# Low parts of the summed output weights written over the sums, four raw buffers in rotation, fewer DVE operations for the activation sums, residual loaded by token tiles

## The chip, the cores and the metric

One core of one Trainium2 chip (trn2) runs the whole block. The metric is the device time in microseconds of one execution; shown is the median of three runs. The engines are named as the profile names them: PE (TensorE), DVE (VectorE), ACT (ScalarE), POOL (GpSimd) and SP (SyncE, here only an issuer of DMAs).

## The reference, cut to what matters

The layer normalises `x` (512 tokens x 2048), projects it, runs two attention branches, gates both, and ends with an output projection, a residual sum and an RMSNorm. The change lies in this last part:

```python
mixed = jnp.concatenate([out_a, out_b], axis=-1)           # 512 x 2048
x = x + jnp.einsum('bsc,cd->bsd', mixed, w_out)            # w_out 2048 x 2048
return rms_norm(x, final_norm_w)
```

All of it is float32. PE gets a float32 product from three faster ones: each operand is split into a high part (rounded) and a low part (the rest), and `hi*hi + hi*lo + lo*hi` is summed. Every operand of PE so costs one copy by ACT (high) and one subtraction by DVE or POOL (low).

## The kernel before, in words

`mixed` is held transposed, 16 tiles of 128 columns x 512 tokens, as eight pairs `j`. The output has 2048 columns. The first 1024 are made plainly: 16 chunks of weights (`WO0 + s`) go through `w_raw`, `w_hi` and `w_lo`, and PE accumulates four token tiles (`out_chunks`, end signalled by `o_done`). The last 1024 columns are made by a product of 2x2 blocks with seven multiplications in place of eight. The operands are sums of blocks:

- of the activations, `unit_sums(j)` (three sums, `u_sum`) and `pair_sums(j)` (two differences, `p_sum`), each then split by `unit_high`/`unit_low` and `pair_high`/`pair_low`;
- of the weights, in 16 **visits** `v`. Visit `v` loads 1 MB, four blocks of 128x512, from `w_pairs` into a raw buffer `t_raw`; `part_sums(v)` (DVE) sums blocks in place (one operation of 128x1024, from visit 8 on one more of 128x512); `part_high(v, g)` (ACT) writes `t_hi`; `part_low(v, g)` (DVE) writes `t_lo`; PE multiplies. Group `g` = 0 is what PE reads first, `g` = 1 what it reads after.

PE takes 18 matmuls in each of visits 0 to 7, 24 in each of 8 to 13, and 48 for the visits 14 and 15 together: 336. In visit 8 it needs the banks that visit 7 has left, so it waits for `y_added`: DVE adds them to the residual `y` in eight operations, `add`, which stand in its order behind `part_low(8, 1)`.

The order on each engine is the order of the code. DVE's is `part_low(v,0)`, `part_sums(v+1)`, `part_low(v,1)`. There are two buffers each of `t_raw`, `t_hi` and `t_lo`. SP loads visit `v` once both low parts of visit `v-2` are made:

```python
for v in range(2, VISITS):
    sp.wait_ge(t_low[0], v - 1)
    sp.wait_ge(t_low[1], v - 1)
    sp.dma_start(t_raw[v % 2][:, :, :], w_pairs[v, :, :, :]).then_inc(t_landed[v % 2], 16)
```

ACT issues the loads of the residual `x_nat` (four of 1 MB, by 512 columns) and of the final gains (`fw`), and squares finished pieces of `y` (`square`). POOL multiplies finished 128x512 pieces of `y` by the gains (`gained`, L393) once they are squared; the first four of these that concern the visits wait for `fws_landed`, all three loads of `fw[1:4]`. At the end DVE adds the last banks, and row by row the norm is applied and stored.

Of the kernel before, what the change touches and what calls it, by code (L numbers as in the profile page):

```python
# [14 lines left out]
P = 128  # L15
# [17 lines left out]
CE = 1024  # L33
# [67 lines left out]
def build(nc, w_stream, w_pairs, x_t, x_nat, gains, final_w, tables, out):  # L101
    with ExitStack() as ctx:
# [10 lines left out]
        def at(name, shape, dt, offset):  # L113
            return nc.alloc_sbuf_tensor_at(name, shape, dt, offset=offset)
# [27 lines left out]
        w_lo = at("w_lo", [P, HL, CE], F32R, r_lo)  # L142
        t_raw = [at("t_raw0", [P, 4, PART], F32, r_x + 56 * KB), at("t_raw1", [P, 4, PART], F32, r_raw)]
        t_hi = [at(f"t_hi{par}", [P, 4, PART], F32R, r_hi + 8 * KB * (1 - par)) for par in range(2)]
        t_lo = [at(f"t_lo{par}", [P, 4, PART], F32R, r_lo + 8 * KB * (1 - par)) for par in range(2)]

# [97 lines left out]
        def part_slots(v, g):  # L244
            return slice(0, 2) if g == 1 else slice(3, 4) if v < 8 else slice(2, 4)

# [17 lines left out]
        y0_landed, y1_landed, y_landed, fw_landed, fws_landed = sem("y0_landed"), sem("y1_landed"), sem("y_landed"), sem("fw_landed"), sem("fws_landed")  # L264
        t_landed = [sem("t_landed0"), sem("t_landed1")]
        u_summed, u_high, u_low, p_summed, p_high, p_low = sem("u_summed"), sem("u_high"), sem("u_low"), sem("p_summed"), sem("p_high"), sem("p_low")
# [25 lines left out]
        def _(sp):  # L292
# [122 lines left out]
        def _(act):  # L415
# [267 lines left out]
            def unit_high(j):  # L683
                act.wait_ge(u_summed, 3 * j + 3)
                act.activation(u_hi[j][:, :, :], u_sum[j % 2][:, :, :], ACT.Copy).then_inc(u_high, 1)

            def pair_high(j):
                act.wait_ge(p_summed, 2 * j + 2)
                act.activation(dead(mx_hi[j]), p_sum[:, j % 2, :, :, :], ACT.Copy).then_inc(p_high, 1)

            def part_high(v, g):

                if g == 0 and v < 8:
                    act.wait_ge(t_landed[v % 2], 16 * (v // 2) + 16)
# [12 lines left out]
                s = part_slots(v, g)  # L707
                act.activation(t_hi[v % 2][:, s, :], t_raw[v % 2][:, s, :], ACT.Copy).then_inc(t_high, 1)  # L708

# [70 lines left out]
        def _(dve):  # L780
# [400 lines left out]
            def unit_sums(j):  # L1181

                if j >= 2:
                    dve.wait_ge(u_low, j - 1)
                even, odd = by_tile(mixed, 2 * j), by_tile(mixed, 2 * j + 1)
                for n, (a, b) in enumerate(((even[:, :, 0, :], odd[:, :, 1, :]), (even[:, :, 1, :], odd[:, :, 1, :]), (even[:, :, 0, :], odd[:, :, 0, :]))):
                    dve.tensor_tensor(u_sum[j % 2][:, n, :].rearrange("p (q c) -> p q c", q=2), a, b, ALU.add).then_inc(u_summed, 1)  # L1187

# [20 lines left out]
            def part_sums(v):  # L1209

                raw = t_raw[v % 2]
                dve.wait_ge(t_landed[v % 2], 16 * (v // 2) + 16)
                dve.tensor_tensor(raw[:, 0:2, :], raw[:, 0:2, :], raw[:, 2:4, :], ALU.subtract if v < 8 else ALU.add).then_inc(t_summed, 1)  # L1213
                if v >= 8:
# [103 lines left out]
            for q in range(2):  # L1318
# [19 lines left out]
        def _(pe):  # L1338
# [523 lines left out]
```

## Time and profile before

| what | value |
|---|---|
| median of 3 runs | 718.03 us (717.88 to 718.6) |
| the profiled execution's own time | 716.37 us |
| its span, first to last instruction | 714.6 us |
| mean granted TensorE clock | 0.979 |
| busy: PE, DVE, ACT, POOL | 93%, 62%, 46%, 38% of the span |

The page cuts the span into 40 slices of 17.9 us. Each digit is the busy share of a slice in tenths (9 is 90% or more), PEclk the granted clock in tenths:

```profile
PE   9999999999999999999999999999999986569853
DVE  5868053896945546455456687765376973457565
PEclk9999999999999999999999999999999999989988
DMA  8633322322222222223223212202462273333315
```

PE is full until slice 32, which ends at 590 us, and has gaps from there on: those are the 16 visits. A "releaser" in a row is what ended an idle time.

### The profile page before, as it was taken

Reading aid. Unit: us, or ns where it says so; the run is one execution under the profiler, and the core shown is the slowest. Engines: PE = TensorE matmul, PEld = TensorE weight load, DVE = VectorE, ACT = ScalarE, POOL = GpSimd, SP = SyncE. Lnnn points to the kernel's source line nnn. Section 1 sums busy time; section 2 is a strip of 40 time slices with the busy share of each in tenths; the row PEclk is TensorE's granted clock in tenths of the full one; section 3 lists DMA queues with packets and bytes.
Section 4 is the critical chain, followed back from the end, with each engine's and each line's share of the span. In section 5 each row is a group of like instructions: output and inputs, shape, how many; then the busy total and the mean of one; then the engine's idle time right before and its main releaser. Section 6 shows DMA issues by size and latency. Waiting matters only on the chain.

```text
span 714.6 us, 8810 instructions
## 1 busy us (share of the span) xinstructions
PE 665.7 (93%) x3126; PEld 553.4 (77%) x3126; DVE 443.8 (62%) x720; ACT 332.0 (46%) x622; POOL 272.6 (38%) x132
## 2 busy tenths in 40 slices
PE   9999999999999999999999999999999986569853
PEld 8888888888888888888888898888888864347642
DVE  5868053896945546455456687765376973457565
ACT  6841232213245636645546676885542341222225
POOL 0054451644344234433342566677747202001001
PEclk9999999999999999999999999999999999989988
DMA  8633322322222222223223212202462273333315
GB/s 288 249 118 99 108 89 88 118 89 91 86 91 87 89 89 88 66 84 117 89 67 110 90 60 89 69 22 88 152 246 71 78 258 139 117 132 143 137 60 236
DMA packets 22169, 81.96 MB, mean 115 GB/s; under 512 B 2417, under 2 KB 2673, under 8 KB 20081
## 3 DMA queue, kind: packets, MB, share of 16 engines
q1 hardware_dynamic: 18000, 73.41, 29.7%
q10 hardware_dynamic: 4128, 8.02, 3.2%
q8 instruction: 25, 0.41, 0.2%
q14 instruction: 16, 0.12, 0.1%
HBM read 77.22 MB, written 4.19 MB: 114 GB/s over the span
## 4 chain that ended last, share of the span: by engine, by line
PE 77%; DVE 11%; DMA 8%; issue 1%; ACT 1%; DVEq 0%; SPq 0%; ACTq 0%
PE bank L1341 23%; PE bank L1344 22%; PE bank L1345 22%; DMA t_raw<-w_pairs 8%; DVE t_lo L1221 3%; DVE t_raw L1213 3%; PE bank L1606 1%; DVE y L1234 1%; DVE u_sum L1187 1%; DVE p_sum L1203 1%; PE bank L1485 1%; PE bank L1495 1%; DVE t_raw L1216 1%; PE bank L1592 1%; PE bank L1593 1%
## 5 line engine op out<-in xcount | busy, mean ns | idle before, releaser
L328 POOL TENSOR_TENSOR w_lo<-w_raw,w_hi 128x1024 fp32r<-128x1024 f32 x84 | 206.0, 2457 | 270.4 <-ACT w_hi L421 270.2
L1341 PE MATMUL bank<-x_hi,w_hi 128*128 128x512 f32 x496 | 193.7, 391 | 0.0
L1344 PE MATMUL bank<-x_hi,w_lo 128*128 128x512 f32 x496 | 193.3, 390 | 0.0
L1345 PE MATMUL bank<-x_lo,w_hi 128*128 128x512 f32 x496 | 193.2, 390 | 0.0
L421 ACT ACTIVATE w_hi<-w_raw 128x1024 fp32r<-128x1024 f32 x93 | 98.2, 1056 | 130.5 <-PE bank L1341 109.0
L1345 PEld LDWEIGHTS bank<-x_lo,w_hi 128*128 128x128 f32 x496 | 93.1, 188 | 19.7
L1341 PEld LDWEIGHTS bank<-x_hi,w_hi 128*128 128x128 f32 x496 | 93.2, 188 | 18.7 <-DVE mixed L1039 0.3
L1344 PEld LDWEIGHTS bank<-x_hi,w_lo 128*128 128x128 f32 x496 | 93.2, 188 | 18.1
L393 POOL TENSOR_TENSOR y<-y,fw 128x512 f32<-128x512 f32 x12 | 18.0, 1519 | 134.2 <-ACT junk L681 108.0
L708 ACT ACTIVATE t_hi<-t_raw 128x1024 fp32r<-128x1024 f32 (+1 forms) x32 | 29.4, 945 | 77.3 <-DVE t_raw L1216 47.7
L1341 PE MATMUL bank<-t_hi,mx_hi 128*128 128x512 f32 x64 | 28.8, 450 | 24.9 <-DVE t_lo L1221 24.9
L1341 PE MATMUL bank<-w_hi,mx_hi 128*128 128x512 f32 x128 | 50.3, 393 | 0.0
L1345 PE MATMUL bank<-w_lo,mx_hi 128*128 128x512 f32 x128 | 49.9, 390 | 0.0
L1344 PE MATMUL bank<-w_hi,mx_lo 128*128 128x512 f32 x128 | 49.9, 390 | 0.0
L1213 DVE TENSOR_TENSOR t_raw<-t_raw 128x1024 f32<-128x1024 f32 x16 | 20.4, 1278 | 43.8 <-DMA t_raw<-w_pairs 43.8
L519 ACT ACTIVATE bank<-pa,st_a 128x128 f32<-128x128 f32 x64 | 22.8, 356 | 43.3 <-DVE st_a L953 43.3
L1341 PEld LDWEIGHTS bank<-t_hi,mx_hi 128*128 128x128 f32 x64 | 13.3, 208 | 32.3 <-DVE t_lo L1221 29.7
L1221 DVE TENSOR_TENSOR t_lo<-t_raw,t_hi 128x1024 fp32r<-128x1024 f32 (+1 forms) x32 | 35.2, 1120 | 4.0 <-ACT t_hi L708 4.0
L968 DVE TENSOR_TENSOR pta_lo<-bank,pta_hi 128x512 fp32r<-128x512 f32 x16 | 11.1, 692 | 32.1 <-ACT pta_hi L526 32.0
L1341 PE MATMUL bank<-t_hi,u_hi 128*128 128x512 f32 x48 | 20.3, 422 | 11.2 <-DVE t_lo L1221 6.5
L1345 PEld LDWEIGHTS bank<-w_lo,mx_hi 128*128 128x128 f32 x128 | 24.0, 188 | 5.0
L856 DVE TENSOR_TENSOR t<-bank,sin_r 32x512 f32<-32x512 f32 x40 | 27.5, 687 | 0.5
(239 smaller groups left out, 1250.5 us busy)
## 6 DMA issues: line engine op xcount, KB each, us to landing
w_raw<-w_stream SPq DMA_DIRECT2D x93, 512.0 KB, 3.3
t_raw<-w_pairs SPq DMA_DIRECT2D x15, 1024.0 KB, 4.8
y<-x_nat ACTq DMA_DIRECT2D x4, 1024.0 KB, 6.0
out<-y SPq DMA_DIRECT2D x8, 512.0 KB, 3.1
xs<-x_t SPq DMA_DIRECT2D x4, 512.0 KB, 5.3
mixed<-x_t SPq DMA_DIRECT2D x4, 512.0 KB, 6.0
t_raw<-w_pairs ACTq DMA_DIRECT2D x1, 1024.0 KB, 7.7
fw<-final_w ACTq DMA_DIRECT2D x4, 256.0 KB, 4.7
```

What stands on the lines that cost most here:

```text
L328: pool.tensor_tensor(w_lo[:, s % HL, :], w_raw[:, s % RAW, :], w_hi[:, s % HL, :].bitcast(F32), ALU.subtract)\
L393: pool.tensor_tensor(y[:, t, cols], y[:, t, cols], fw[n][:, :], ALU.mult).then_inc(o_gained, 1)
L421: act.activation(w_hi[:, s % HL, :], w_raw[:, s % RAW, :], ACT.Copy).then_inc(w_hi_ready, 1)
L519: act.activation(B[4][:, P * k:P * k + P], pa[:, slot, k, :], ACT.Exp, bias=st[:, 1, k:k + 1], scale=A_SCALE, accum_out=st[:, 3, k:k + 1])
L708: act.activation(t_hi[v % 2][:, s, :], t_raw[v % 2][:, s, :], ACT.Copy).then_inc(t_high, 1)
L856: ins = dve.tensor_tensor(t2[32 * q:32 * q + 32, :], src[32 * o:32 * o + 32, :], sin[32 * q:32 * q + 32, :], ALU.mult)
L968: dve.tensor_tensor(pta_lo[:, :], B[6][:, :], pta_hi[:, :].bitcast(F32), ALU.subtract).then_inc(a_pt_lo, 1)
L1213: dve.tensor_tensor(raw[:, 0:2, :], raw[:, 0:2, :], raw[:, 2:4, :], ALU.subtract if v < 8 else ALU.add).then_inc(t_summed, 1)
L1221: dve.tensor_tensor(t_lo[v % 2][:, s, :], t_raw[v % 2][:, s, :], t_hi[v % 2][:, s, :].bitcast(F32), ALU.subtract).then_inc(t_low[g], 1)
L1341: ins = pe.matmul(dst, ah, bh, start=start, stop=False, skip_group_check=goes_on)
L1344: pe.matmul(dst, al, bh, start=False, stop=False, skip_group_check=goes_on)
L1345: return pe.matmul(dst, ah, bl, start=False, stop=stop, skip_group_check=goes_on)
```

## The change: what it does

- **Raw buffers.** `t_raw` has four buffers. `t_lo` has four as well, and each lies on the bytes of the `t_raw` of the same number: the low part is written over the sum it is made from. `t_hi` keeps two. To make that fit, the sums are written into blocks 2 and 3, and the order of blocks in `w_pairs` is changed on the host; two `add` operations become subtractions.
- **Loads of the visits.** SP loads visit 2 when PE has begun chunk 14 of the plain part, visit 3 when PE has ended the plain part, and visit `v` from 4 on when PE has ended visit `v-4`.
- **Activation sums.** `unit_sums` is two operations (128x512 with a broadcast operand, and 128x256) in place of three of 128x256; `pair_sums` is one of 128x512 in place of two of 128x256.
- **Residual.** The second half of the columns is loaded by pairs of token tiles: tiles 2 and 3 behind `unit_high(2)`, tiles 0 and 1 where both loads stood.
- **Final gains.** ACT issues the three loads of `fw[1:4]` behind `part_high(6, 1)`; they stood behind `part_high(1, 1)`.

```diff
-        t_raw = [at("t_raw0", [P, 4, PART], F32, r_x + 56 * KB), at("t_raw1", [P, 4, PART], F32, r_raw)]
+        t_at = [r_x + 56 * KB, r_raw, r_lo + 8 * KB, r_lo]
+        t_raw = [at(f"t_raw{n}", [P, 4, PART], F32, o) for n, o in enumerate(t_at)]
+        t_lo = [at(f"t_lo{n}", [P, 4, PART], F32R, o) for n, o in enumerate(t_at)]
...
-            for v in range(2, VISITS):
-                sp.wait_ge(t_low[0], v - 1)
-                sp.wait_ge(t_low[1], v - 1)
-                sp.dma_start(t_raw[v % 2][:, :, :], w_pairs[v, :, :, :]).then_inc(t_landed[v % 2], 16)
+            sp.wait_ge(w_used, WO0 + 14)
+            sp.dma_start(t_raw[2][:, :, :], w_pairs[2, :, :, :]).then_inc(t_landed[2], 16)
+            sp.wait_ge(o_done, 8)
+            sp.dma_start(t_raw[3][:, :, :], w_pairs[3, :, :, :]).then_inc(t_landed[3], 16)
+            for v in range(4, VISITS):
+                if v == 11:
+                    sp.wait_ge(m_done, 6)
+                else:
+                    sp.wait_ge(t_used, 2 * v - 6 if v < 11 else 2 * v - 8)
+                sp.dma_start(t_raw[v % 4][:, :, :], w_pairs[v, :, :, :]).then_inc(t_landed[v % 4], 16)
...
+            def residual_rows(t):
+                act.dma_start(y[:, t:t + 2, CE:], x_nat[0, P * t:P * t + 2 * P, CE:].rearrange("(t p) d -> p t d", p=P)).then_inc(y_landed, 16)
...
             unit_high(2)
+            residual_rows(2)
             high_part(WO0 + 10, WO0 + 10)
...
             act.wait_ge(u_low, 8)
-            residual_in(2, y_landed)
-            residual_in(3, y_landed)
+            residual_rows(0)
             part_high(1, 0)
             pair_high(7)
             part_high(1, 1)
-            act.wait_ge(p_low, 8)
-            for n in range(1, 4):
-                act.dma_start(fw[n][:, :], final_w[:, SEQ * n:SEQ * n + SEQ]).then_inc(fws_landed, 16)
...
                 part_high(v, 0)
                 part_high(v, 1)
+                if v == 6:
+                    act.wait_ge(p_low, 8)
+                    for n in range(1, 4):
+                        act.dma_start(fw[n][:, :], final_w[:, SEQ * n:SEQ * n + SEQ]).then_inc(fws_landed, 16)
...
-                    dve.tensor_tensor(u_sum[j % 2][:, n, :].rearrange("p (q c) -> p q c", q=2), a, b, ALU.add).then_inc(u_summed, 1)
+                dve.tensor_tensor(u_sum[j % 2][:, 0:2, :].rearrange("p n (q c) -> p n q c", q=2), even.rearrange("p q e c -> p e q c"),
+                                  odd[:, :, 1, :].unsqueeze(1).to_broadcast([P, 2, 2, P]), ALU.add).then_inc(u_summed, 1)
+                dve.tensor_tensor(u_sum[j % 2][:, 2, :].rearrange("p (q c) -> p q c", q=2), even[:, :, 0, :], odd[:, :, 0, :], ALU.add).then_inc(u_summed, 1)
...
-                dve.tensor_tensor(p_sum[:, j % 2, 0, :, :], even[:, :, 1, :], even[:, :, 0, :], ALU.subtract).then_inc(p_summed, 1)
-                dve.tensor_tensor(p_sum[:, j % 2, 1, :, :], odd[:, :, 0, :], odd[:, :, 1, :], ALU.subtract).then_inc(p_summed, 1)
+                both = mixed[:, 2 * j:2 * j + 2, :].rearrange("p k (q e c) -> p k q e c", q=2, e=2)
+                dve.tensor_tensor(p_sum[:, j % 2, :, :, :], both[:, :, :, 1, :], both[:, :, :, 0, :], ALU.subtract).then_inc(p_summed, 1)
```

What the edits do to the order is seen at three places. The first is SP's queue where the visits' loads begin, before (`t_low0`, `t_low1` count the low parts of groups 0 and 1 made by DVE):

```order
L308 ISA [waits w_lo_ready]
L308 DMA w_raw<-w_stream 128x1024
...
L311 DMA t_raw_61<-w_pairs 128x2048 [waits w_lo_ready]
L315 DMA t_raw_60<-w_pairs 128x2048 [waits t_low1,t_low0]
L315 DMA t_raw_61<-w_pairs 128x2048 [waits t_low1,t_low0]
```

and now (`t_used` counts the groups PE has ended; 60 to 63 are the raw buffers):

```order
L312 DMA t_raw_61<-w_pairs 128x2048 [waits w_lo_ready]
L314 DMA t_raw_62<-w_pairs 128x2048 [waits w_used]
L316 DMA t_raw_63<-w_pairs 128x2048 [waits o_done]
L322 DMA t_raw_60<-w_pairs 128x2048 [waits t_used]
L322 DMA t_raw_61<-w_pairs 128x2048 [waits t_used]
L322 DMA t_raw_62<-w_pairs 128x2048 [waits t_used]
```

The number and order of the loads are as before; what each waits for has changed from DVE to PE, two visits further back. The second place is ACT's order at the visits 1 and 2, before:

```order
L671 DMA y<-x_nat 128x4x512 x2
L708 ACTIVATE t_hi_63<-t_raw_61 128x512
L689 ACTIVATE mx_hi_134<-p_sum 128x2x2x128
L708 ACTIVATE t_hi_63<-t_raw_61 128x1024
L748 DMA fw_165<-final_w 128x512
L748 DMA fw_166<-final_w 128x512
L748 DMA fw_167<-final_w 128x512
L681 ACTIVATE junk,sumsq<-y 128x512 x4
```

and now, down to visits 6 and 7:

```order
L681 DMA y<-x_nat 128x2x1024
L718 ACTIVATE t_hi_69<-t_raw_61 128x512
L699 ACTIVATE mx_hi_138<-p_sum 128x2x2x128
L718 ACTIVATE t_hi_69<-t_raw_61 128x1024
L691 ACTIVATE junk,sumsq<-y 128x512 x4
...
L718 ACTIVATE t_hi_68<-t_raw_62 128x1024
L765 DMA fw_169<-final_w 128x512
L765 DMA fw_170<-final_w 128x512
L765 DMA fw_171<-final_w 128x512
L718 ACTIVATE t_hi_69<-t_raw_63 128x512
```

One load of the residual has left this place, and the three loads of the gains stand five visits later. The third is DVE's order while PE is in the plain part, before (the sums of pair 2 and of unit 4, then their low parts):

```order
L1202 TENSOR_TENSOR p_sum<-mixed 128x256
L1203 TENSOR_TENSOR p_sum<-mixed 128x256
L1187 TENSOR_TENSOR u_sum_145<-mixed 128x256 x3
L1207 TENSOR_TENSOR mx_lo_137<-p_sum,mx_hi_129 128x2x2x128
L1191 TENSOR_TENSOR u_lo_160<-u_sum_145,u_hi_152 128x768
```

and now:

```order
L1214 TENSOR_TENSOR p_sum<-mixed 128x512
L1197 TENSOR_TENSOR u_sum_149<-mixed 128x512
L1199 TENSOR_TENSOR u_sum_149<-mixed 128x256
L1218 TENSOR_TENSOR mx_lo_141<-p_sum,mx_hi_133 128x2x2x128
L1203 TENSOR_TENSOR u_lo_164<-u_sum_149,u_hi_156 128x768
```

Five sums of one place are now three; nothing has changed its turn.

## Rows read from the trace of the kernel before

**Rows 1.** The page, chain that ended last, shares of the span by engine.

```profile
PE 77%; DVE 11%; DMA 8%; issue 1%; ACT 1%; DVEq 0%; SPq 0%; ACTq 0%
```

**Rows 2.** Busy time by stretch (stretch, length, engines, PEclk, DMA share, GB/s).

```profile
577.40:702.90 125.50, 89.39 (x337) 67.82 (x336) 73.88 (x85) 38.75 (x55) 10.83 (x7) 0.90 0.40 142
590.00:600.00 10.00, 4.62 (x15) 3.40 (x14) 4.04 (x3) 1.69 (x2) 4.76 (x4) 0.83 0.32 120
```

**Rows 3.** Waits from 577.6 to 702.9 us (in total, times, longest).

```profile
DVE t_raw L1213 <- DMA t_raw<-w_pairs: 43.8, 12, 4.4
...
PE bank L1341 <- DVE t_lo L1221: 31.4, 14, 5.4
```

**Rows 4.** The chain in order of time (start, length, what), in the visits.

```profile
585.29 7.10 DMA t_raw<-w_pairs
...
603.13 4.84 DMA t_raw<-w_pairs
608.00 1.23 DVE t_raw L1213
609.22 1.15 DVE t_lo L1221
```

**Rows 5.** PE's instructions in order of time (start, length, idle before).

```profile
577.21 0.39 PE L1345 MATMUL bank<-w_lo,mx_hi 128*128 128x512 f32 x1
...
582.21 0.50 PE L1341 MATMUL bank<-t_hi,u_hi 128*128 128x512 f32 x1 [0.53 <-DVE t_lo L1221]
...
585.27 0.50 PE L1341 MATMUL bank<-t_hi,mx_hi 128*128 128x512 f32 x1 [1.40 <-DVE t_lo L1221]
...
588.86 0.50 PE L1341 MATMUL bank<-t_hi,u_hi 128*128 128x512 f32 x1 [0.58 <-DVE t_lo L1221]
...
595.90 0.80 PE L1341 MATMUL bank<-t_hi,mx_hi 128*128 128x512 f32 x1 [5.38 <-DVE t_lo L1221]
...
598.99 0.40 PE L1344 MATMUL bank<-t_hi,mx_lo 128*128 128x512 f32 x1
...
642.12 0.80 PE L1341 MATMUL bank<-t_hi,u_hi 128*128 128x512 f32 x1 [4.67 <-DVE y L1234]
...
697.02 0.39 PE L1345 MATMUL bank<-t_lo,mx_hi 128*128 128x512 f32 x1
...
702.46 0.39 PE L1345 MATMUL bank<-t_lo,mx_hi 128*128 128x512 f32 x1
```

**Rows 6.** Instructions on `t_raw`: ns min/median/max, first and last start.

```profile
L1221 DVE TENSOR_TENSOR t_lo<-t_raw,t_hi x32: 678/1218/2296, 570.5 to 690.4; 128x1024 fp32r<-128x1024 f32 x24, 128x512 fp32r<-128x512 f32 x8
L1213 DVE TENSOR_TENSOR t_raw<-t_raw x16: 1218/1226/2090, 564.2 to 686.2; 128x1024 f32<-128x1024 f32 x16
...
L1216 DVE TENSOR_TENSOR t_raw<-t_raw x8: 691/692/1664, 631.2 to 687.5; 128x512 f32<-128x512 f32 x8
```

**Rows 7.** DVE's instructions in order of time.

```profile
578.41 2.48 DVE L1226 TENSOR_TENSOR y<-bank,y 128x512 f32<-128x512 f32 x4
...
640.79 4.87 DVE L1234 TENSOR_TENSOR y<-y,bank 128x512 f32<-128x512 f32 x8
...
652.80 2.09 DVE L1213 TENSOR_TENSOR t_raw<-t_raw 128x1024 f32<-128x1024 f32 x1 [0.66 <-DMA t_raw<-w_pairs]
654.92 1.66 DVE L1216 TENSOR_TENSOR t_raw<-t_raw 128x512 f32<-128x512 f32 x1
```

**Rows 8.** POOL's instructions in order of time.

```profile
588.75 6.01 POOL L393 TENSOR_TENSOR y<-y,fw 128x512 f32<-128x512 f32 x4 [26.18 <-DMA fw<-final_w]
652.52 3.52 POOL L393 TENSOR_TENSOR y<-y,fw 128x512 f32<-128x512 f32 x2 [57.76 <-ACT junk L681]
699.85 1.30 POOL L393 TENSOR_TENSOR y<-y,fw 128x512 f32<-128x512 f32 x1 [43.82 <-ACT junk L681]
```

**Rows 9.** ACT's instructions and DMA issues in order of time.

```profile
539.85 1.06 ACT L421 ACTIVATE w_hi<-w_raw 128x1024 fp32r<-128x1024 f32 x1 [3.33 <-PE bank L1341]
...
582.98 1.31 ACTq L748 DMA_DIRECT2D fw<-final_w  x3
```

More of the change, by code:

```diff
@@ L244, in part_slots @@
         def part_slots(v, g):
-            return slice(0, 2) if g == 1 else slice(3, 4) if v < 8 else slice(2, 4)
+            return slice(2, 4) if g == 1 else slice(1, 2) if v < 8 else slice(0, 2)
         def dead(mx):
@@ L264, in build @@
         y0_landed, y1_landed, y_landed, fw_landed, fws_landed = sem("y0_landed"), sem("y1_landed"), sem("y_landed"), sem("fw_landed"), sem("fws_landed")
-        t_landed = [sem("t_landed0"), sem("t_landed1")]
+        t_landed = [sem(f"t_landed{n}") for n in range(4)]
         u_summed, u_high, u_low, p_summed, p_high, p_low = sem("u_summed"), sem("u_high"), sem("u_low"), sem("p_summed"), sem("p_high"), sem("p_low")
@@ L683, in unit_high @@
             def unit_high(j):
-                act.wait_ge(u_summed, 3 * j + 3)
+                act.wait_ge(u_summed, 2 * j + 2)
                 act.activation(u_hi[j][:, :, :], u_sum[j % 2][:, :, :], ACT.Copy).then_inc(u_high, 1)
             def pair_high(j):
-                act.wait_ge(p_summed, 2 * j + 2)
+                act.wait_ge(p_summed, j + 1)
                 act.activation(dead(mx_hi[j]), p_sum[:, j % 2, :, :, :], ACT.Copy).then_inc(p_high, 1)
@@ L693, in part_high @@
                 if g == 0 and v < 8:
-                    act.wait_ge(t_landed[v % 2], 16 * (v // 2) + 16)
+                    act.wait_ge(t_landed[v % 4], 16 * (v // 4) + 16)
                 else:
@@ L707, in part_high @@
                 s = part_slots(v, g)
-                act.activation(t_hi[v % 2][:, s, :], t_raw[v % 2][:, s, :], ACT.Copy).then_inc(t_high, 1)
+                act.activation(t_hi[v % 2][:, s, :], t_raw[v % 4][:, s, :], ACT.Copy).then_inc(t_high, 1)
             act.sem_inc(o_squared, 1)
@@ L1209, in part_sums @@
             def part_sums(v):
[L1211 to L1214, printed above, removed]
+                raw = t_raw[v % 4]
+                dve.wait_ge(t_landed[v % 4], 16 * (v // 4) + 16)
+                if v < 8:
+                    dve.tensor_tensor(raw[:, 2:4, :], raw[:, 0:2, :], raw[:, 2:4, :], ALU.subtract).then_inc(t_summed, 1)
+                else:
+                    dve.tensor_tensor(raw[:, 2:4, :], raw[:, 2:4, :], raw[:, 0:2, :], ALU.add).then_inc(t_summed, 1)
                     dve.wait_ge(t_summed, 2 * v - 7)
-                    dve.tensor_tensor(raw[:, 2, :], raw[:, 2, :], raw[:, 3, :], ALU.add).then_inc(t_summed, 1)
+                    dve.tensor_tensor(raw[:, 0, :], raw[:, 0, :], raw[:, 1, :], ALU.add).then_inc(t_summed, 1)
             def part_low(v, g):
                 dve.wait_ge(t_high, 2 * v + g + 1)
+                if g == 0 and v < 8:
+                    dve.wait_ge(t_summed, v + 1)
                 s = part_slots(v, g)
-                dve.tensor_tensor(t_lo[v % 2][:, s, :], t_raw[v % 2][:, s, :], t_hi[v % 2][:, s, :].bitcast(F32), ALU.subtract).then_inc(t_low[g], 1)
+                dve.tensor_tensor(t_lo[v % 4][:, s, :], t_raw[v % 4][:, s, :], t_hi[v % 2][:, s, :].bitcast(F32), ALU.subtract).then_inc(t_low[g], 1)
             def residual(n, t):
@@ L1292, in _ @@
             for q in range(2):
-                add(2 * q + 1, 2, q, q + 5, 2 * q + 1)
+                add(2 * q + 1, 2, q, q + 5, 2 * q + 1, op=ALU.subtract)
             part_low(9, 0)
@@ L1330, in _ @@
                     scaled(0, 1, 3, 9)
-                add(2 * q, 2, q, d + 4, b + 5)
+                add(2 * q, 2, q, d + 4, b + 5, op=ALU.subtract)
             scaled(2, 3, 3, 10)
@@ L1697, in m @@
             def m(v, q, bk, s, slot, start=False):
-                return three(B[bk + q][:, :], *s, t_hi[v % 2][:, slot, :], t_lo[v % 2][:, slot, :], start, v in (7, 15), goes_on=v >= 8 and bk in (0, 6))
+                return three(B[bk + q][:, :], *s, t_hi[v % 2][:, slot, :], t_lo[v % 4][:, slot, :], start, v in (7, 15), goes_on=v >= 8 and bk in (0, 6))
             def m1(v, q):
-                return m(v, q, 4, s1(v - 8, q), 2, v == 8)
+                return m(v, q, 4, s1(v - 8, q), 0, v == 8)
             def m5(v, q):
-                return m(v, q, 2, s5(v - 8, q), 3, v == 8)
+                return m(v, q, 2, s5(v - 8, q), 1, v == 8)
             def m6(v, q):
-                return m(v, q, 6, s_kept(v - 8, q, 0, 1), 0)
+                return m(v, q, 6, s_kept(v - 8, q, 0, 1), 2)
             def m7(v, q):
-                return m(v, q, 0, s_kept(v - 8, q, 1, 0), 1)
+                return m(v, q, 0, s_kept(v - 8, q, 1, 0), 3)
             for v in range(8):
@@ L1717, in _ @@
                 for q in range(2):
-                    ins = m(v, q, 4, s2(v, q), 3, v == 0)
+                    ins = m(v, q, 4, s2(v, q), 1, v == 0)
                     if v == 7:
@@ L1726, in _ @@
                 for q in range(2):
-                    ins = m(v, q, 6, s_kept(v, q, 0, 0), 0, v == 0)
+                    ins = m(v, q, 6, s_kept(v, q, 0, 0), 2, v == 0)
                     if v == 7:
@@ L1732, in _ @@
                 for q in range(2):
-                    ins = m(v, q, 0, s_kept(v, q, 1, 1), 1, v == 0)
+                    ins = m(v, q, 0, s_kept(v, q, 1, 1), 3, v == 0)
                     if v == 7:
@@ L1816, in laid_out_pairs @@
     blocks = w_out[:, 2 * SEQ:].reshape(8, 2, P, 2, SEQ)
-    order = [((0, 1), (1, 0), (1, 1), (0, 0)), ((0, 1), (1, 0), (0, 0), (1, 1))]
+    order = [((0, 1), (0, 0), (1, 1), (1, 0)), ((0, 0), (1, 1), (0, 1), (1, 0))]
     return np.ascontiguousarray(np.concatenate([np.stack([blocks[:, k, :, n, :] for k, n in o], axis=2) for o in order], axis=0))
```

3 lines of the change are left out of this document (removed).

## The prediction

> **What bounds the kernel now.** I read the chain first: PE carries 77% of it, DVE 11% and DMA 8% [rows 1]. Eight per cent of 714.6 us is 57 us in which the end waited for a load, and the slices say where: PE is full up to about 580 us and has gaps behind. So next the busy times by stretch. From 577.4 to 702.9 us, the visits, PE is busy 89.39 of 125.5 us at a granted clock of 0.90, over 337 matmuls, one of them the last of the plain part [rows 2]: 36 us idle, and part of the rest run slowly. The waits name the cause: 31.4 us of PE's waits are for `t_lo`, and DVE itself waited 43.8 us for loads of `t_raw` [rows 3].
>
> The chain in order of time shows the loop: a load of 4.84 us, a sum of 1.23 us, a low part of 1.15 us, then the next load [rows 4]. With two buffers and DVE's order (sum of visit v+1 ahead of the second low part of visit v) a visit takes all three in a row, 7.3 us; from visit 8 on there is one more sum of 0.69 us [rows 6] and it takes 7.9. PE needs less. In the last stretch 24 steps from 697.02 to 702.46 us take 5.44 us, 0.2267 us a matmul [rows 5]: 18 matmuls are 4.08 us, 24 are 5.44. The visits are bound by the load's latency, not by its bandwidth.
>
> **The floor.** PE's visits start where its last plain matmul ends, 577.21 + 0.23 = 577.44 us [rows 5]. 336 matmuls x 0.2267 = 76.2 us. Before, PE ended at 702.46 + 0.39 = 702.85 us [rows 5], 125.4 us after its start: 49.2 us are waits and slow clock. That is all that can be had in the visits. The 11.75 us from PE's end to the end of the span (last adds, norms, stores) are not touched by the change and I keep them.
>
> **Four raw buffers.** Let PE end visit v at T. The load of visit v+4 goes out, lands at T+4.9, its sum is made by T+6.1, then the second low part of visit v+3 by T+7.3. PE starts visit v+3 at T+8.2 and wants that low part at T+9.5. Slack 2.2 us. In the visits from 8 on, the sums end at T+6.9 and the low part at T+8.1, wanted at T+13.6: slack 5.5. DVE has 1.23 + 0.69 + 1.22 = 3.1 us of work for a visit of 4.08 us, then 1.23 + 0.69 + 2 x 1.22 = 4.4 us for 5.44 [rows 6]. `t_hi` still has two buffers: from PE's end of a group ACT needs 1.06 and DVE 1.22 us, 2.4 in all with the signals, and PE comes back to that group 5.4 us later. So in the steady state nothing waits and PE sets the pace: 16 visits cost the 76.2 us. What is late next is what stands between the visits. In the order of time:
>
> 1. *Start.* Before, PE waited 0.53 + 1.40 + 0.58 = 2.5 us here [rows 5], since DVE reached the four residual sums at 578.41 us and ended them at 580.9 [rows 7], 3.4 us behind PE's last plain matmul. Three of the four can be made before PE ends; so DVE can gain up to 3.4 - 0.8 = 2.6 us, and no less than 0. Eight pairs and eight units lose an operation each on the way there, and an operation that meets one of POOL costs about 1 us more (1.66 in place of 0.69 us, [rows 7, 6], beside POOL's two of 652.52, [rows 8]); POOL makes low parts all along this stretch. I take DVE 1.5 us earlier. ACT, too, issues one load less and squares without first issuing the gains (1.31 us, [rows 9]). Waits left: 1.0 us, between 0 and 2.5.
>
> 2. *Visit 8.* Let T be the start of visit 7. Sums of visit 8, low parts (7,1) and (8,0) are made by T+1.2; the load of visit 9 has landed at T+0.8, its sums end at T+3.0, the low part (8,1) at T+4.2, and then come eight adds in 4.87 us [rows 7]. PE wants the second at T+5.4: it is there. The fourth costs it 0.5, visit 9's low part 0.2. That is 0.7 us in place of the 4.67 us that it waited here before [rows 5].
>
> 3. *POOL in the way.* The three loads of gains used to be issued at 583 us, so POOL's four products ran from 588.75 us for 6.01 us [rows 8], when DVE was waiting for a load. Now ACT issues them behind the high part (6,1), which waits for PE's end of visit 4 and takes the 1.06 us of a copy of this size [rows 9]. The issues take 1.31 us and the landing 588.75 - 584.29 = 4.5 us more, together 6.9 us after visit 4, or 1.3 us before visit 7. POOL then works beside DVE in the very stretch of step 2 where DVE has no slack. What a POOL product costs DVE, two rows show: a sum took 2.09 in place of 1.23 us and one 1.66 in place of 0.69 while POOL ran two products [rows 7, 8], 1.83 us for two, so 3.7 us for four. I take 3.7. Bounds: 0, if they fall into a pause, and 6.0, if each costs DVE all that a product takes beside other work (6.01/4 = 1.5 us).
>
> The Trainium skill, "SBUF — State Buffer", section "Who interferes with whom", says that a DVE instruction with two SBUF inputs and a POOL instruction that reads SBUF exclude each other for a whole instruction. By that rule four products of 1.30 us, the uncontended row, would cost 5.2 us and the end would come 1.5 us later than by the rows; the adds of step 2 (one input from PSUM) would go free. The trace agrees with the blocking, and shows 0.9 us per product, not 1.3.
>
> 4. *Visit 10.* Two more products of POOL behind the squares. DVE has 1 us of slack there and loses 1.8: 1.0 us, between 0 and 2.
>
> 5. *Visits 14 and 15.* PE reaches group 1 of visit 15 after only 12 matmuls of the pair; its high part must wait for the end of visit 13, and high and low part need 2.4 us, of which 1.36 are covered by PE. 1.2 us wait.
>
> 6. *Clock.* After the gap of 5.38 us PE ran the next 7 matmuls in 598.99 - 595.90 = 3.09 us in place of 1.59 [rows 5], in a stretch with granted clock 0.83 [rows 2], so partly at the lower of the two levels (1.2 GHz in place of 2.4). One gap of about 4 us is left, at visit 8: 1.5 us. Between 0 and 3.4.
>
> **Costs at nothing.** The early half of the residual (1 MB at about 527 us) can delay chunk loads. But at 539.85 ACT waits 3.33 us for PE to free a chunk's place, not for a load [rows 9]: the chunks are ahead. Without that cover it would cost a load's length, 5 us at most. The other half, visit 3's load and visit 4's are 3 MB within 4 us. The load of 7.10 us at 585.29 shows such a crowd [rows 4]; visit 3 is wanted 10 us and visit 4 9 us after issue. Writing a low part over its sum: L1213 writes in place already, at 1.226 us median against 1.218 for L1221, which does not [rows 6]. The flipped signs and the 4 KB runs of the residual: same operations, same bytes.
>
> **The sum.** 76.2 + 1.0 + 0.7 + 3.7 + 1.0 + 1.2 + 1.5 = 85.3 us of visits, against 125.4. PE ends at 662.7, the span is 662.7 + 11.75 = 674.5, 40.1 us less than 714.6. The execution's own time of 716.37 becomes 676.3; the median of the runs lies 1.66 us above it, 718.03, and becomes 677.9 us.
>
> **Rivals.**
> - *POOL does not touch DVE's path.* For it: before, the four products of 588.75 us lay in a pause of DVE, which waited for the load that ended at 592.4 [rows 4, 8]. Against: that pause is what the change takes away. Steps 3, 4 and 6 fall: 677.9 - 6.2 = 671.7; with half of step 4 kept, 672.
> - *Loads get slower.* Now up to three are under way, and each row of 4.84 us was alone. If one takes the 7.10 us of the crowded row, the slack of 2.2 us in visits 3 to 8 is gone, visit 9's load lands at T+3.1 and the adds are 2.3 us late; if in turn they only run one behind the other at 4.84 against PE's 4.08, seven visits lose 0.76 each, 5.3 less the slack of 2.2. Both come to about +3, 681. Against: 142 GB/s over the stretch [rows 2], and 1 MB in 4.08 us is 257.
> - *DVE becomes the bound, and the kernel slower.* Low parts written over their own input, with a broadcast operand and PE reading the same lines, could run slower than the two-buffer form. DVE's work in the visits is 8 x 3.1 + 8 x 4.4 = 60 us plus 4.9 of adds. To use up 125.4 us its operations must take 2.0 times as long; at 2.1 times it is 131 us and the time 723. For it: factors of 1.7 to 2.4 do occur, beside POOL. Against: POOL is busy 10.8 us in the whole stretch, and in-place costs nothing in rows 6.
> - *The buffers free nothing*, because `t_hi` still has two: excluded by 2.4 against 5.4 us above, so I give it next to nothing; it would be 718.
>
> **Chances.** My forecast 0.58; POOL harmless 0.22; slower loads 0.17; no change 0.01; slower 0.02. The bounds of the steps give 677.9 - 7.2 = 670.7 below (1.0, 3.7, 1.0 and 1.5 all gone) and, above, +1.5 for the start, +2.3 for POOL, +1 for visit 10, +1.9 for the clock and +2 for loads: 686.6. This takes in the first two rivals. Faster by over 0.2% (about what a measurement of this kernel can tell from no change): 0.97; within: 0.01; slower: 0.02.
>
> **What would show it.** Right: DVE's waits for `t_raw` loads fall from 43.8 us to under 10; PE's for `t_lo` from 31.4 to under 5; in visits 3 to 7 no PE gap, a visit each 4.1 us, from 8 on each 5.4 to 5.5; a gap of 3 to 5 us in visit 8 released by DVE's `y`, beside four POOL products; clock at 1.00 but behind that gap; loads issued at PE's visit ends. Wrong: gaps in every visit, loads above 7 us, DVE operations on `t_raw` above 1.3 us without POOL, or a tail after PE's end that is not 11.75 us.

## The result, and the profile after

| | before | after |
|---|---|---|
| median | 717.95 us (717.27 to 718.6, 4 runs) | 678.08 us (677.9 to 678.47, 4 runs) |
| the profiled execution's own time, its span | 716.37, 714.6 us | 678.47, 676.7 us |
| PE's visits, first matmul to the end of the last | 577.44 to 702.85 us | 577.91 to 665.03 us |

The ratio is 0.9445 (95%: 0.9429 to 0.9462). Forecast were 677.9 us.

The slices of the page after, now 16.9 us each, and its chain that ended last:

```profile
PE   9999999999999999999999999999999999997993
DVE  5958031978784635645544578777545489879975
PEclk9999999999999999999999999999999999997997
DMA  8732222233122212222321412202127523683516
...
PE 87%; DVE 7%; issue 2%; ACT 2%; DMA 1%; DVEq 0%; ACTq 0%
```

PE carries 87% of the chain in place of 77%, and DMA 1% in place of 8% [rows 1]. One slice, the 37th, is left with a visible gap.

The stretch of the visits but for its last 2 us, and the 20 us around that gap (columns as in [rows 2]):

```profile
577.40:663.00 85.60, 79.27 (x331) 63.42 (x331) 73.28 (x78) 37.37 (x52) 12.63 (x7) 0.96 0.51 185
610.00:620.00 10.00, 5.93 (x22) 4.46 (x22) 9.96 (x10) 2.00 (x2) 5.27 (x3) 0.86 0.53 182
620.00:630.00 10.00, 10.00 (x37) 7.99 (x36) 8.80 (x10) 3.35 (x6) 1.40 (x1) 0.79 0.29 107
```

DVE has 73 us of work in both kernels [rows 2], once in 125.5 us and now in 85.6. The waits in this stretch (in total, times, longest):

```profile
PE bank L1356 <- DVE y L1249: 4.1, 1, 4.1
DVE t_raw L1225 <- DMA t_raw<-w_pairs: 2.6, 2, 1.4
DVE t_raw L1227 <- DMA t_raw<-w_pairs: 2.4, 1, 2.4
PE bank L1356 <- DVE t_lo L1236: 2.1, 3, 1.1
```

DVE's waits for loads are 5.0 us in place of 43.8, PE's for `t_lo` 2.1 in place of 31.4 [rows 3]. All of PE's idle times of 0.2 us and more in the visits:

```profile
583.74 0.50 PE L1356 MATMUL bank<-t_hi,mx_hi 128*128 128x512 f32 x1 [0.23 <-DVE t_lo L1236]
...
609.75 0.50 PE L1356 MATMUL bank<-t_hi,mx_hi 128*128 128x512 f32 x1 [0.79 <-DVE t_lo L1236]
...
618.20 0.79 PE L1356 MATMUL bank<-t_hi,u_hi 128*128 128x512 f32 x1 [4.07 <-DVE y L1249]
...
655.19 0.50 PE L1356 MATMUL bank<-t_hi,mx_hi 128*128 128x512 f32 x1 [1.11 <-DVE t_lo L1236]
```

How the gap at 618.20 comes about, in the chain of waits (start, length, what), in DVE's rows and in POOL's:

```profile
599.47 6.01 DMA t_raw<-w_pairs
```
```profile
605.51 1.23 DVE L1227 TENSOR_TENSOR t_raw<-t_raw 128x1024 f32<-128x1024 f32 x1 [2.37 <-DMA t_raw<-w_pairs]
...
607.38 4.54 DVE L1236 TENSOR_TENSOR t_lo<-t_raw,t_hi 128x1024 fp32r<-128x1024 f32 x2
611.85 2.31 DVE L1227 TENSOR_TENSOR t_raw<-t_raw 128x1024 f32<-128x1024 f32 x1
614.19 1.63 DVE L1229 TENSOR_TENSOR t_raw<-t_raw 128x512 f32<-128x512 f32 x1
615.74 1.21 DVE L1236 TENSOR_TENSOR t_lo<-t_raw,t_hi 128x1024 fp32r<-128x1024 f32 x1
616.88 4.86 DVE L1249 TENSOR_TENSOR y<-y,bank 128x512 f32<-128x512 f32 x8
```
```profile
607.23 8.04 POOL L400 TENSOR_TENSOR y<-y,fw 128x512 f32<-128x512 f32 x4 [44.59 <-DMA fw<-final_w]
```

The load for visit 8 is late (6.01 us), then DVE's operations that start from 607.38 to 614.19 are long: these are the ones beside POOL's four products. Behind the gap PE is slow for 14 matmuls, of which these are two:

```profile
618.79 0.63 PE L1359 MATMUL bank<-t_hi,u_lo 128*128 128x512 f32 x1
619.22 0.63 PE L1360 MATMUL bank<-t_lo,u_hi 128*128 128x512 f32 x1
```

They start 0.43 us apart, up to 623.91 us, in place of 0.23. The granted clock of this stretch is 0.50, the lower of the two levels (1.2 GHz):

```profile
618.20:624.00 5.80, 5.80 (x14) 4.47 (x15) 5.80 (x9) 0.00 (x0) 0.00 (x0) 0.50 0.01 3
```

### The profile page after: what moved, and what is told of

The parts are those of the page before. It is cut to its first block, busy times and chain, and to the rows that moved or that the text cites. A ratio compares the mean times of both kernels' runs of the same rounds, so it can differ in the third digit from the quotient of the medians.

```text
span 676.7 us, 8788 instructions
## 1 busy us (share of the span) xinstructions
PE 657.6 (97%) x3126; PEld 550.7 (81%) x3126; DVE 442.1 (65%) x704; ACT 332.2 (49%) x622; POOL 274.9 (41%) x132
## 4 chain that ended last, share of the span: by engine, by line
PE 87%; DVE 7%; issue 2%; ACT 2%; DMA 1%; DVEq 0%; ACTq 0%
PE bank L1356 26%; PE bank L1359 26%; PE bank L1360 26%; DVE t_lo L1236 2%; PE bank L1621 1%; PE bank L1500 1%; PE bank L1510 1%; DMA t_raw<-w_pairs 1%; DVE y L1249 1%; DVE p_sum L1214 1%; ACT junk L691 1%; DVE u_lo L1203 1%; PE bank L1386 1%; PE bank L1607 1%; PE bank L1608 1%
## 5 line engine op out<-in xcount | busy, mean ns | idle before, releaser
L400 POOL TENSOR_TENSOR y<-y,fw 128x512 f32<-128x512 f32 x12 | 20.6, 1738 | 94.2 <-ACT junk L691 49.6
L1236 DVE TENSOR_TENSOR t_lo<-t_raw,t_hi 128x1024 fp32r<-128x1024 f32 (+1 forms) x32 | 37.3, 1187 | 5.3 <-ACT t_hi L718 5.3
L1356 PE MATMUL bank<-t_hi,mx_hi 128*128 128x512 f32 x64 | 26.2, 410 | 2.3 <-DVE t_lo L1236 2.1
L1356 PEld LDWEIGHTS bank<-w_hi,mx_hi 128*128 128x128 f32 x128 | 24.0, 188 | 4.7
L1359 PEld LDWEIGHTS bank<-w_hi,mx_lo 128*128 128x128 f32 x128 | 24.1, 188 | 4.6
L987 DVE TENSOR_TENSOR mixed<-bank,o_low 64x256 f32<-64x256 f32 x32 | 13.5, 422 | 21.6 <-ACT o_low L540 21.4
```

The costliest lines, as they stand in the source:

```text
L400: pool.tensor_tensor(y[:, t, cols], y[:, t, cols], fw[n][:, :], ALU.mult).then_inc(o_gained, 1)
L987: ins = dve.tensor_tensor(out_e, by_head[h, e], o_low[h, :, :, :], ALU.add)
L1236: dve.tensor_tensor(t_lo[v % 4][:, s, :], t_raw[v % 4][:, s, :], t_hi[v % 2][:, s, :].bitcast(F32), ALU.subtract).then_inc(t_low[g], 1)
L1356: ins = pe.matmul(dst, ah, bh, start=start, stop=False, skip_group_check=goes_on)
L1359: pe.matmul(dst, al, bh, start=False, stop=False, skip_group_check=goes_on)
```

## The experiments

In the table "waits" are PE's idle times in the visits that the profile puts down to another engine (0.15 us and more). "Slow" are the matmuls that start 0.3 to 0.7 us after the one before them without such a wait, with what they take beyond 0.2267 us each, and the last column has those among them that lie in or right behind a stretch with a granted clock of 0.50. Most of the others are the second matmul behind a wait: it starts 0.33 to 0.35 us after the first, at a granted clock of 1.00, and so costs 0.11 us. All this is worked out from PE's rows of the one profiled execution. The ratio is to the runs of before on the same chip.

| kernel | median | ratio (95%) | visits | waits | slow | of these, clock |
|---|---|---|---|---|---|---|
| before | 717.95 | 1 | 125.4 | 36.1 | 54: 10.1 | 42: 8.8 |
| after | 678.08 | 0.9445 (0.9429 to 0.9462) | 87.1 | 6.2 | 20: 3.7 | 14: 2.9 |
| e1 buffers only | 678.06 | 0.9447 (0.9429 to 0.9466) | 86.1 | 7.1 | 9: 1.0 | 0 |
| e2 gains early | 677.05 | 0.9425 (0.9401 to 0.9448) | 86.8 | 6.5 | 16: 2.5 | 8: 1.6 |
| e3 gains late | 675.0 | 0.9405 (0.9388 to 0.9422) | 83.2 | 4.6 | 8: 0.9 | 0 |
| e4 no products | 675.59 | 0.9406 (0.9386 to 0.9426) | 84.6 | 4.5 | 16: 2.6 | 9: 1.6 |
| e5 order, two buffers | 689.36 | 0.9601 (0.9579 to 0.9622) | 98.5 | 15.1 | 29: 5.4 | 21: 4.5 |
| e6 sums only | 716.51 | 0.9981 (0.997 to 0.9993) | 125.4 | 33.2 | 68: 12.9 | 59: 12.0 |
| e7 three buffers | 688.78 | 0.9598 (0.9577 to 0.9618) | 97.9 | 13.4 | 36: 6.4 | 24: 4.9 |
| e8 paced products | 672.77 | 0.9387 (0.9358 to 0.9415) | 81.4 | 2.3 | 11: 1.5 | 0 |
| e9 paced, order swapped | 680.48 | 0.9481 (0.9459 to 0.9503) | 88.7 | 7.8 | 20: 3.6 | 15: 3.0 |

**e1: the four buffers alone.** Before, with SP's rotation and the low parts over the sums; the sums of the activations, the residual and the place of the gains' loads stay as they were.

```diff
-        t_raw = [at("t_raw0", [P, 4, PART], F32, r_x + 56 * KB), at("t_raw1", [P, 4, PART], F32, r_raw)]
+        t_raw = [at(f"t_raw{n}", [P, 4, PART], F32, o) for n, o in enumerate(t_at)]
+        t_lo = [at(f"t_lo{n}", [P, 4, PART], F32R, o) for n, o in enumerate(t_at)]
```

> Only the four raw buffers with the low parts over the sums and the loads at PE's visit ends; the activation sums, the residual loads and the place of the gains' loads are those of before. Theory (the buffers carry the gain; the late gains cost something that the other edits give back): 76.2 us of matmuls, 2.5 of waits at the start, about 1.5 where POOL's four products now meet the low slack of visits 3 and 4, 0.7 at visit 8, 1.0 and 1.2 at visits 10 and 15, no slow clock: PE ends 42 us earlier than before, 674 to 679 us. Rival (the activation sums and the residual carry a good part): 683 us or more.

678.06 us, the same as after and in the theory's range. So the buffers are enough for the whole gain, and the other edits add up to nothing that the runs can tell. They do not do nothing: the start here waits as before (0.53, 1.41 and 0.58 us, [rows 5], and 0.62 more in visit 2) where after waits 0.23, and visits 4 and 10 wait 0.74 and 1.92 us where after doesn't. Against that, visits 7 and 8 cost 0.22 us where after waits 4.86 and then runs at the lower clock for 2.9. What the other edits gain at the start, the later loads of the gains take back. The edit of the residual was never run by itself.

**e2 and e3: the gains' loads earlier and later.** After, with the three loads of `fw` where they were before (behind `part_high(1, 1)`), and, in e3, behind visit 11.

```diff
-                if v == 6:
+                if v == 11:
```

> The changed kernel with the three loads of the gains back behind part_high(1,1). Theory (at visit 8 it is POOL's products and the crowded load that hold DVE up): the gap of 4.07 us at visit 8 falls to about 0.7, the slow clock behind it (14 matmuls at 0.43 us, 2.8 us) goes, and POOL costs up to 1.5 us at visits 3 and 4: 671 to 674 us. Rival (DVE's own order, low part and eight adds, makes the gap): visit 8 keeps over 3 us and the time stays at 677 to 680.

> The changed kernel with the three loads of the gains behind part_high(11,1). Theory (as for the early place, and DVE has 5.5 us of slack a visit from 10 on): no gap at visit 8 over 1 us, none made at visits 12 to 14: 670 to 673 us, below the early place. Rival (POOL's six products then run into the tail, where the products are waited for): over 677 us.

Both fell short of what was expected. POOL's products of e2, and PE beside them:

```profile
590.70 7.93 POOL L400 TENSOR_TENSOR y<-y,fw 128x512 f32<-128x512 f32 x4 [28.18 <-DMA fw<-final_w]
```
```profile
599.77 0.50 PE L1355 MATMUL bank<-t_hi,mx_hi 128*128 128x512 f32 x1 [1.75 <-DVE t_lo L1235]
...
631.26 0.50 PE L1355 MATMUL bank<-t_hi,mx_hi 128*128 128x512 f32 x1 [1.95 <-DVE t_lo L1235]
```

Visit 8 waits 0.23 us, as expected, but the products in a row now cost 1.75 us at visit 4, and visit 10 waits 1.95 us, which after doesn't. In e3 all six products run in one row, beside visits 11 to 13:

```profile
631.19 11.82 POOL L400 TENSOR_TENSOR y<-y,fw 128x512 f32<-128x512 f32 x6 [69.15 <-DMA fw<-final_w]
```
```profile
644.14 0.50 PE L1356 MATMUL bank<-t_hi,mx_hi 128*128 128x512 f32 x1 [2.23 <-DVE t_lo L1236]
...
649.49 0.50 PE L1356 MATMUL bank<-t_hi,u_hi 128*128 128x512 f32 x1 [1.65 <-DVE t_lo L1236]
```

The damage moves with the products. The median of e2 can't be told from after's (the intervals of the ratios overlap), and it lies in the rival's range although the rival's gap at visit 8 is not there. e3 is 3.1 us below after, with intervals that don't overlap: the place matters, even with six products in a row.

**e4: without the four products.** After, but POOL only signals; columns 512 to 1023 of the output lack their final gain.

```diff
-                gained(t, 1)
+                pool.sem_inc(o_gained, 1)
```

> The changed kernel; POOL leaves out the four products of the second column quarter by the gains (output columns 512 to 1023 lack the final gain). The loads of the gains stay behind part_high(6,1). Theory (the four products cost DVE about 4 us, which all come out as PE's wait): the gap of 4.07 us falls to 1 to 1.5 us, the rest being the load of visit 8 that takes 6.0 in place of 4.8 us beside the loads of the gains; with the slow clock 672 to 674 us. Rival (the gap is the crowded load's alone): the gap stays above 3 us, 677 us.

```profile
613.65 0.50 PE L1356 MATMUL bank<-t_hi,u_hi 128*128 128x512 f32 x1 [1.01 <-DVE y L1249]
614.85 0.50 PE L1356 MATMUL bank<-t_hi,u_hi 128*128 128x512 f32 x1 [0.23 <-DVE y L1249]
...
628.78 0.50 PE L1356 MATMUL bank<-t_hi,mx_hi 128*128 128x512 f32 x1 [1.95 <-DVE t_lo L1236]
```

The waits up to visit 8 are now 1.24 us in place of 4.86 (0.79 in visit 7 and 4.07 in visit 8): the four products cost PE 3.6 us. What is left follows the load of visit 8: with 1.24 us of waits here it takes 6.02 us beside the gains' loads, and where these stand elsewhere, in e2 and e3, it takes 4.7 us and the visit waits 0.23 and 0.21. So 1.0 of the 1.24 us is the crowded load. The expected time was missed because the wait of visit 10 comes back, as in e2: the two other products start at 624.04 us, and the gap in which DVE had got ahead is missing.

**e5: DVE's order with two buffers.** Before, with only this edit (the same in the loop from visit 10 on):

```diff
                 part_low(v, 0)
-                part_sums(v + 1)
                 part_low(v, 1)
+                part_sums(v + 1)
```

> The kernel before, with two raw buffers; the only edit is DVE's order in the visits: both low parts of visit v, then the sums of visit v+1. Theory A (it is the order that puts load, sum and low part in one row; a buffer's own round of load 4.8, sum 1.2, high 1.1 and low 1.2 us is 8.3 us for two visits): visits 3 to 7 run at 4.1 to 4.5 us, the later ones at 5.5 to 6.0, and the time is 676 to 684 us, most of the gain without a third buffer. Theory B (the buffers are what it takes, the loads start too late with two): a visit keeps 7 us and more, over 705 us.

689.36 us, above what A expected and far below B. 28 of the 40 us come without a byte more of buffers: the second low part no longer waits for the next load, so two loads are under way at a time. DVE's rows in its later visits:

```profile
627.11 2.35 DVE L1221 TENSOR_TENSOR t_lo<-t_raw,t_hi 128x1024 fp32r<-128x1024 f32 x2
...
632.45 2.36 DVE L1221 TENSOR_TENSOR t_lo<-t_raw,t_hi 128x1024 fp32r<-128x1024 f32 x2 [1.13 <-ACT t_hi L708]
```

A round of sums, ACT's high part and two low parts takes 5.34 us (632.45 - 627.11), just under PE's 5.44. What is left to the four buffers are single events: one wait of 3.37 us behind a load that took 8.19 beside those of the residual and the gains, 2.44 us at visit 8, one of 1.58, one of 5.25 us at the end behind a load of 6.33, and 4.5 us of lower clock, behind the longest two. The waits of the start (2.5 us) are no matter of buffers, since e1 has them too.

**e6: only the fewer sums.** Before, with `unit_sums` and `pair_sums` of after. One of the seven block products enters part of the columns with the other sign; the operations are the same.

> The kernel before with the activation sums in fewer operations and nothing else. Theory (the visits of before are one chain of loads that starts when DVE ends low part (1,1); DVE is 1.4 us earlier in the changed kernel at the residual sums, 576.95 against 578.41): the whole chain moves by 1.3 to 1.6 us, 716.4 to 717 us. Rival (the operations are off the path): within 0.3 us of before.

```profile
577.19 1.28 DVE L1226 TENSOR_TENSOR y<-bank,y 128x512 f32<-128x512 f32 x2
```
```profile
595.68 0.79 PE L1341 MATMUL bank<-t_hi,mx_hi 128*128 128x512 f32 x1 [6.44 <-DVE t_lo L1221]
```

DVE is 1.22 us earlier than in [rows 7], and the start loses its waits but for 0.24 and 0.57; the next wait is 6.44 us in place of 5.38 [rows 5]. While the loads set the pace, most of what is gained at the start is waited for at the first late load: that wait ends only 0.22 us earlier (595.68 against 595.90). The time, 716.51 us and a ratio of 0.9981, is 0.2% below before and in the theory's range, but a chain that moves as a whole by 1.3 us is not in the trace; more matmuls at the lower clock (12.0 us against 8.8) blur the comparison of the two profiled executions.

**e7: three buffers.** After, with a load behind PE's end of visit v-3.

```diff
-        t_at = [r_x + 56 * KB, r_raw, r_lo + 8 * KB, r_lo]
+        t_at = [r_x + 56 * KB, r_raw, r_lo + 8 * KB]
```

> The changed kernel with three raw buffers in place of four: visit v is loaded at PE's end of visit v-3. Theory (slack by buffer: low part (v+2,1) is made 7.3 us after PE's end of v-1, wanted after 5.4 in visits 3 to 7 and after 8.2 later): 1.9 us of wait in each of visits 3 to 7, 6.0 us a visit, none from 9 on; with the gap at visit 8 partly swallowed 683 to 689 us. Rival (loads have more slack than computed, three do): 677 to 679. Rival (crowded loads of 6 us): over 692.

The chain in order of time:

```profile
581.69 4.79 DMA t_raw<-w_pairs
...
586.50 1.22 DVE t_raw L1224
587.72 1.15 DVE t_lo L1235
...
588.91 0.50 PE bank L1355
```

From a load's issue to PE's first matmul are 7.2 us. PE covers 24 matmuls of it (5.4 us), and waits 1.3 us in visits 2 and 4 (588.91, 599.17), then 2.1 in visit 6 and 3.6 in visit 7, beside the gains' loads (6.6 us for one of 1 MB) and POOL's products. The time is in the expected range; the form is not, since 1.9 us in each of visits 3 to 7 and none from 9 on were expected, and visits 10 and 14 wait 1.93 and 2.98. That four buffers leave some slack and three leave less than none is borne out. The size, 2.2 us with four and a visit of 4.1 us for each buffer, stays an estimate.

**e8: paced products.** After, with the gains' loads behind visit 2 and each product held until PE has ended a certain visit (2, 3, 4, 10, 11, 12).

```diff
+                pool.wait_ge(t_used, (6, 8, 10, 20)[t])
...
+                pool.wait_ge(t_used, (22, 24)[q])
...
-                if v == 6:
+                if v == 2:
```

> The changed kernel; the loads of the gains stand behind part_high(2,1), and each of POOL's six products waits for PE's end of a visit of its own (2, 3, 4, 10, 11, 12), so that two never follow each other and none lies between visits 5 and 9. Theory (each visit leaves DVE about 1 us idle, one product costs about 1 us, so none of them reaches PE): gaps at visits 8 and 10 under 0.5 us each, only the 1.1 us of visit 15 left, PE's visits in 80 to 82 us against 87.1: 671 to 673 us, below all runs so far. Rival (waits move elsewhere whatever the place of the products): 675 us as with the late gains.

Three of POOL's six rows, and PE's longest waits:

```profile
590.99 1.38 POOL L400 TENSOR_TENSOR y<-y,fw 128x512 f32<-128x512 f32 x1 [28.83 <-PE bank L1362]
595.04 2.10 POOL L400 TENSOR_TENSOR y<-y,fw 128x512 f32<-128x512 f32 x1 [2.67 <-PE bank L1362]
599.22 2.02 POOL L400 TENSOR_TENSOR y<-y,fw 128x512 f32<-128x512 f32 x1 [2.07 <-PE bank L1362]
```
```profile
613.61 0.50 PE L1358 MATMUL bank<-t_hi,u_hi 128*128 128x512 f32 x1 [0.56 <-DVE y L1251]
...
647.83 0.50 PE L1358 MATMUL bank<-t_hi,u_hi 128*128 128x512 f32 x1 [1.13 <-DVE t_lo L1238]
```

The products no longer reach PE: 2.3 us of waits are left, all at clock 1.00, and the kernel takes 672.77 us, 5.3 less than after (0.6% by the ratios, whose intervals don't overlap). It is the fastest of all here. The 0.79 us at visit 8 miss the expected 0.5; its load took 5.5 us, behind three of about 7 that the gains' loads had crowded. Against e3 the gain is 2.2 us, which the intervals can't tell, so how much of the 5.3 is the pacing and how much the place is not shown.

**e9: the paced kernel with DVE's order swapped**, by the edit of e5.

> The paced kernel with DVE's order swapped as well: it writes low(v,0) and low(v,1) one behind the other and then sums visit v+1, instead of summing between them. Theory A (with four buffers DVE has more slack than the order needs, so the order of its work is free now): PE's waits stay at about 2 us, the span at 669 to 672, the median 671 to 674, no change against the paced kernel that can be told. Theory B (the chain from the sums through ACT's high part to the low part, 5.35 us a visit where DVE ran in this order with two buffers, bounds the later visits, which PE does in about 5.3): waits of 0.3 to 1 us at five or more of the later visits, the span 674 to 680, the median 675 to 682.

```profile
637.12 1.22 DVE L1229 TENSOR_TENSOR t_raw<-t_raw 128x1024 f32<-128x1024 f32 x1
...
643.44 2.31 DVE L1229 TENSOR_TENSOR t_raw<-t_raw 128x1024 f32<-128x1024 f32 x1
...
649.89 1.22 DVE L1229 TENSOR_TENSOR t_raw<-t_raw 128x1024 f32<-128x1024 f32 x1
```
```profile
654.23 0.80 PE L1358 MATMUL bank<-t_hi,u_hi 128*128 128x512 f32 x1 [4.38 <-DVE t_lo L1238]
```

680.48 us is in B's range. The form differs from what B expected: not five small waits but 2.21 us at visit 8, 0.73 at 648.89 and 4.38 at the end. A round is 5.35 us bare, and 6.32 and 6.45 beside a product (643.44 - 637.12, 649.89 - 643.44). With 0.1 us of slack against PE's 5.44 nothing of this is made good, and it comes due in visits 14 and 15. So the order that won 28 us with two buffers loses 7.7 with four (6.7 by the ratios, the two having run on different chips).

## Why the prediction was right, point by point

The sum of the visits, term by term (after, one profiled execution):

| step | expected | measured |
|---|---|---|
| 336 matmuls | 76.2 | 76.2 |
| 1, start | 1.0 | 0.2 |
| 2 and 3, visit 8 with POOL's four products | 0.7 + 3.7 | 4.9 (0.79 + 4.07) |
| 4, visit 10 | 1.0 | 0 |
| 5, visit 15 | 1.2 | 1.1 |
| 6, clock | 1.5 | 2.9 |
| first and second matmul behind each wait, and rest | 0 | 1.8 |
| visits | 85.3 | 87.1 |

- **The mechanism**, slack against the load's latency, held: no idle time of 0.2 us between 583.74 and 609.75 us, DVE's and PE's waits below the bounds named, e7 for the sign of the slack. Both rivals that dispute it, DVE as the bound and buffers that free nothing, are refuted.
- **Start.** DVE begins the four residual adds at 576.95 us, 1.46 earlier than in [rows 7]; 1.5 was forecast. PE waits 0.2 us rather than 1.0. That the fewer sums bring DVE forward, e1 and e6 show together. They leave waits of 0.57 us (e6) and 0.59 and 0.61 (e2) in visit 2, which are gone only where ACT doesn't issue the gains' loads there.
- **POOL in the way.** DVE loses 4.1 us to the four products by its own rows (4.54 in place of 2.44 in e4, 2.31 in place of 1.22, 1.63 in place of 0.69), PE 3.6 us by e4, against 3.7. *POOL does not touch DVE's path* is refuted. By the exclusive lock of the Trainium skill ("SBUF — State Buffer", "Who interferes with whom") each product would cost its whole length, 5.2 us as an estimate. The trace agrees that the two hold each other up and again shows less, 0.9 to 1.1 us for each. The adds, with one input from PSUM, were not put to the test in after, where the products had ended when they began. The trace of before has such operations: this one of DVE, with an input from PSUM, lies wholly within one of POOL's and takes the 0.69 us that its like take with POOL idle.

```profile
204.76 0.69 DVE L968 TENSOR_TENSOR pta_lo<-bank,pta_hi 128x512 fp32r<-128x512 f32 x1 [3.80 <-ACT pta_hi L526]
```
```profile
203.21 2.40 POOL L328 TENSOR_TENSOR w_lo<-w_raw,w_hi 128x1024 fp32r<-128x1024 f32 x1
```
- **Visit 8 by itself** costs 0.2 us (e2, e3), not 0.7, and 1.2 with its load at 6.01 us in place of 4.8 beside the gains' three loads, issued 0.1 us behind it (e4). This is the rival of slower loads, for 1.0 us of PE's time. It holds for more loads than this one: those of visits 3, 9 and 10 took 6.2, 6.1 and 7.5 us, and cost nothing, since DVE waits for none of them. A load above 7 us was named as a sign of being wrong, and here it was none.
- **Visit 10** cost nothing, for a reason that the prediction missed: the gap at visit 8 stops PE but not DVE, which gets ahead. Where the gap is gone (e2, e4) the wait stands there with 1.95 us. The steps were added as if they were independent, and they are not.
- **Clock**: mis-sized, though within its bounds. Behind the gap of 4.07 us 14 matmuls were slow, 2.9 us; behind the 5.38 us of [rows 5] it had been 7.
- **The start behind a wait**: a term that the sum lacks. Apart from the wait itself and from the clock, the first matmul behind a wait comes 0.16 us later than in a full stream and the second 0.11 (609.75 and 655.19 us, granted clock 1.00). With four waits and a step of 0.51 us at 588.26, for which the profile names no wait, this is most of the 1.8 us.
- **The end.** From PE's end to the end of the span are 11.67 us, against 11.75.

The span came out at 676.7 us, 2.2 above the 674.5 of the sum: 1.8 from the visits, and 0.5 since they began at 577.91 us in place of 577.44. The median fits to 0.2 us all the same, because the profiled execution of after is 0.4 us above its median where that of before was 1.66 below: so much of the agreement is luck, and so is that within the visits the clock and the starts behind waits (3.2 us too little in the sum) were in part offset by the start and visit 10 (1.8 too much). What remains open is which gaps bring the lower clock. Every stretch at 0.50 within the visits of these traces begins in a gap of PE or within 2.5 us behind one, the shortest of 1.93 us (e7). But gaps of 2.92 and 3.02 us in before, 2.23 in e3 and 1.92 in e1 brought none.

## What to carry to other kernels

Where a loop is bound by a load's latency, count what one more buffer gives in units of a step against the time from issue to first use, and look for the instruction that ties the loads to each other: moving it gave 28 of the 40 us without memory. Decide the order of the engine in between again after the buffers: the same order that won with two lost 7.7 us with four. Side work on POOL that holds DVE up, and side loads that crowd the loop's own, belong where there is slack: late and in a row they cost 3.1 us less than in the tightest stretch, one operation a step 5.3 less. And waits are not a sum, since a gap on one engine is a lead for another.

## What the runs showed of the hardware that was not expected

- A 1 MB load of 4.8 us took 6.0 with three loads of 256 KB issued just behind it, and the next two, 4 and 8 us later, took 6.1 and 7.5. In e5 one took 8.19 beside the loads of the residual and the gains.
- A POOL product of 128x512 takes 1.38 us where DVE leaves room and 1.75 to 2.16 beside it (e8), and a DVE operation on SBUF beside one 0.9 to 1.1 us more. A DVE operation with an input from PSUM took 0.69 us with and without POOL at work (before).
- The number of slow matmuls behind a gap does not follow its length: 14 behind 4.07 us, 7 behind 5.38.
